# Where the weight tiles of the first outputs of a stage lie relative to h: other distances for gate/up and for queries, keys and values

## What is computed

```
for l in range(2):
    x = x + 0.5 * swiglu(rms_norm(x), wg1, wu1, wd1)      # wide: 2816
    h = rms_norm(x)
    z = h @ w_in                                          # q, k, v and three convolution parts
    x = x + concat(sliding_window_attention(q, k, v), short_conv(...)) @ w_out
    x = x + 0.5 * swiglu(rms_norm(x), wg2, wu2, wd2)
x = rms_norm(x)
```

## Time and profile before

| what | value |
|---|---|
| median of 3 launches | 1254.28 us |
| the three launches | 1238.87, 1262.2 and 1254.28 us |
| the profiled execution, its own time | 1245.92 us |
| its span, first to last instruction | 1244.1 us |
| mean granted clock of TensorE | 0.993 |
| TensorE matmuls, busy | 1202.5 us (97%) |
| TensorE weight loads, busy | 1161.1 us (93%) |
| VectorE, ScalarE, GpSimd busy | 816.5, 656.4 and 166.0 us |
| read from memory | 208.91 MB |

### The profile page before, as it was taken

One profiled execution on the slowest core, in us unless ns is written; L12 is line 12 of the kernel. 1 busy time (PEld: TensorE's weight loads), 2 busy tenths in 40 slices (PEclk: granted clock), 3 DMA queues, 4 the chain that ended last, 5 costly groups with the idle time before them and its releaser, 6 DMA issues.

```text
span 1244.1 us, 27307 instructions
## 1 busy us (share of the span) xinstructions
PE 1202.5 (97%) x10002; PEld 1161.1 (93%) x10002; DVE 816.5 (66%) x1390; ACT 656.4 (53%) x1121; POOL 166.0 (13%) x228
## 2 busy tenths in 40 slices
PE   6999999999999999999999999999997999998998
PEld 6999999799999999999999799999996887998888
DVE  6766654768666654777665868677656666655664
ACT  5454543556545544555543646555545665655652
POOL 3000000342000000000000351000000000401960
PEclk9999999999999999999999999999997999999999
DMA  7655753455555753655743446556652430543542
GB/s 281 200 180 191 230 175 113 143 166 191 184 187 185 239 166 117 202 189 189 252 167 136 136 159 196 190 195 216 212 169 75 137 126 20 168 155 128 179 153 86
DMA packets 56742, 210.91 MB, mean 170 GB/s; under 512 B 7200, under 2 KB 9280, under 8 KB 56544
## 3 DMA queue, kind: packets, MB, share of 16 engines
q1 hardware_dynamic: 54048, 203.45, 49.3%
q0 software_dynamic: 2480, 6.48, 1.8%
q10 hardware_dynamic: 144, 0.06, 0.0%
HBM read 208.91 MB, written 1.05 MB: 169 GB/s over the span
## 4 chain that ended last, share of the span: by engine, by line
PE 84%; DVE 7%; ACT 3%; issue 3%; POOL 2%; DMA 0%; DVEq 0%; ACTq 0%; SPq 0%
PE bank L1173 25%; PE bank L1175 25%; PE bank L1174 25%; DVE w_lo L748 3%; PE bank L1211 2%; PE bank L1520 2%; PE bank L1500 1%; DVE h_lo L767 1%; ACT w_hi L457 1%; PE bank L1485 1%; DVE probs L886 1%; PE bank L1422 1%; PE bank L1424 1%; PE bank L1423 1%; PE bank L1480 1%
## 5 line engine op out<-in xcount | busy, mean ns | idle before, releaser
L1173 PE MATMUL bank<-h_hi,w_hi 128*128 128x256 f32 (+1 forms) x1992 | 566.8, 285 | 16.8 <-DVE w_lo L748 11.6
L1175 PE MATMUL bank<-h_hi,w_lo 128*128 128x256 f32 (+1 forms) x1992 | 557.9, 280 | 0.0
L1174 PE MATMUL bank<-h_lo,w_hi 128*128 128x256 f32 (+1 forms) x1992 | 557.8, 280 | 0.0
L748 DVE TENSOR_TENSOR w_lo<-w_raw,w_hi 128x1024 fp32r<-128x1024 f32 (+1 forms) x360 | 467.7, 1303 | 75.1 <-ACT w_hi L457 74.9
L457 ACT ACTIVATE w_hi<-w_raw 128x1024 fp32r<-128x1024 f32 (+1 forms) x360 | 397.1, 1108 | 75.9 <-PE bank L1175 58.3
L1173 PEld LDWEIGHTS bank<-h_hi,w_hi 128*128 128x128 f32 x1992 | 377.1, 189 | 24.0 <-issue 19.4
L1175 PEld LDWEIGHTS bank<-h_hi,w_lo 128*128 128x128 f32 x1992 | 379.9, 191 | 0.0
L1174 PEld LDWEIGHTS bank<-h_lo,w_hi 128*128 128x128 f32 x1992 | 377.3, 189 | 0.9
L1173 PE MATMUL bank<-g_hi,w_hi 128*128 128x256 f32 x832 | 232.5, 279 | 1.5 <-DVE g_lo L893 0.8
L1174 PE MATMUL bank<-g_lo,w_hi 128*128 128x256 f32 x832 | 231.7, 278 | 0.0
L1175 PE MATMUL bank<-g_hi,w_lo 128*128 128x256 f32 x832 | 231.7, 278 | 0.0
(11 more groups left out here) (152 smaller groups left out, 1159.5 us busy)
## 6 DMA issues: line engine op xcount, KB each, us to landing
w_raw<-in_w SPq DMA_DIRECT2D x296, 512.0 KB, 3.3
w_raw<-in_wd SPq DMA_DIRECT2D x64, 704.0 KB, 4.1
w_raw<-in_relbias POOLq DMA_DIRECT2D x64, 64.0 KB, 2.3
btab_sb<-in_btab POOLq DMA_DIRECT2D x1, 1536.0 KB, 9.3
x_res<-in_xT SPq DMA_DIRECT2D x2, 512.0 KB, 4.9
out_T<-x_res SPq DMA_DIRECT2D x8, 128.0 KB, 1.7
rope_sb<-in_rope POOLq DMA_DIRECT2D x1, 272.0 KB, 3.9
mats_sb<-in_mats POOLq DMA_DIRECT2D x1, 192.0 KB, 3.8
```

What stands on the lines that cost most here:

```text
L748: dve.tensor_tensor(wlo[:, slot, at:at + cols], raw[:, slot, 0:cols], whi[:, slot, at:at + cols].bitcast(F32), ALU.subtract).then_inc(lo_r ...
L1173: pe.matmul(o, h, xh, start=first, stop=False)
L1174: pe.matmul(o, h, xl, start=False, stop=False)
L1175: return pe.matmul(o, lo, xh, start=False, stop=last)
```

## The change

The single shift `ASIDE` becomes a table by stage and output. `first_pair` is told which stage it works for, and output 2 of `gu1` and `gu2` is shifted too, at its splits and at its matmuls. The second block reads its first slots with the shifts of `gu1`.

```diff
-ASIDE = 56
+ASIDE = {('gu1', 1): 8, ('gu1', 2): 56, ('gu2', 1): 48, ('gu2', 2): 56, ('qkv', 1): 16}
 def tile_at(phase, i):
-    return ASIDE if phase in ("gu1", "gu2", "qkv") and i == 1 else 0
+    return ASIDE.get((phase, i), 0)
...
-            def first_pair(ready, q):
+            def first_pair(name, ready, q):
...
-                        mm = product(bank[o][:, 0:T], o, k, *hcols(k), k == 0, k == KT - 1, at=o * ASIDE)
+                        mm = product(bank[o][:, 0:T], o, k, *hcols(k), k == 0, k == KT - 1, at=tile_at(name, o))
...
-                            product(bank[1][:, 0:T], 1, k1, *hcols(k1), k1 == 0, False, at=ASIDE)
+                            product(bank[1][:, 0:T], 1, k1, *hcols(k1), k1 == 0, False, at=tile_at(name, 1))
...
-                first_pair(lambda r: ready(r, 0), q)
+                first_pair(name, lambda r: ready(r, 0), q)
                 for r in (2, 3):
                     ready(r, 0)
-                    tile8(bank[r][:, 0:T], r)
+                    tile8(bank[r][:, 0:T], r, at=tile_at(name, r))
...
-                                             at=a * ASIDE)
+                                             at=tile_at("gu1", a))
...
-                        mm = product(o[:, 0:TOKENS[kind]], slot, i, *hcols(i, TOKENS[kind]), i == 0, i == KT - 1)
+                        mm = product(o[:, 0:TOKENS[kind]], slot, i, *hcols(i, TOKENS[kind]), i == 0, i == KT - 1,
+                                     at=tile_at("gu1", 2) if piece == 2 else 0)
```

More of the change, by code:

```diff
@@ L1251, in qkv @@
             def qkv(l, q):
-                first_pair(lambda i: pe.wait_ge(lo_ready[PHASES["qkv"].slot(i)], uses("qkv", i, l)), q)
+                first_pair("qkv", lambda i: pe.wait_ge(lo_ready[PHASES["qkv"].slot(i)], uses("qkv", i, l)), q)
                 for i in range(2, QKV):
```

## The result

| | before | changed |
|---|---|---|
| median of 20 launches | 1249.98 us | 1250.02 us |
| lowest and highest | 1237.96, 1262.2 | 1245.16, 1261.93 |
| launches up to 1240 us | 5 | 0 |
| 1244 to 1248.2 us | 5 | 10 |
| 1251.8 to 1254.9 us | 7 | 9 |

What follows compares the result with a forecast made beforehand. TensorE, busy 97% of the span, was taken to be bound by the pace of matmul starts. From the profiled 1245.92 us, 13.6 off for all four stretches fast and 0.5 added for output 2 gave 1232.8, forecast as 1233 us; range 1229 to 1256.

Steps and rivals of the forecast that it cites:

- the two paces: Gate/up/down stretches from output 2 on: the same matmuls run at 0.1131 or 0.1176 us each, kept throughout the stretch.
- the price of a stretch: One slow gate/up/down stretch of 1536 matmuls costs 6.8 us over a fast one (180.70 against 173.90 us).
- the new second tile: Output 1 at 160, 0 or 128 bytes: if even, it fixes each stage's pace; bounds -13.6 to +13.6 us.
- all four (or all but a rare one) fast: Main case: all four gate/up/down stretches take the fast pace, giving 1233 us; chance 0.47.
- all slow: Rival: the regular handover leads to the slow pace in all four stretches, 1260.0 us; chance 0.09 for all or nearly all.
- gu1 as regular: Start of gu1: with output 1 even at its new distance, the handover comes in the same moment every time.
- One kind fixed fast, the other slow or open: Rival on gu1 and gu2: with two slow stretches 1246.4 us, with one 1239.6; chance 0.14.
- The draw stays a draw: Rival: nothing is fixed, each stretch is slow in 10 of 16 cases, 1249.8 us; chance 0.25.
- a slow window: Sign of being wrong: a window from output 3 on at 178 us in place of 171 us.
- the splits: ScalarE and VectorE writing the shifted tile at another address: taken as 0, with room to hide slower writes.
- the loads: Loads run at 196 to 201 GB/s in both paces, so they don't hold up a faster stretch.
- the waits: TensorE in the first block is hardly ever short of work; its two longest wait totals are 5.7 and 2.6 us.

Runs made afterwards that it cites:

- no_third: Changed kernel with the third tile of gu1 and gu2 back at 192 bytes; median 1256.69 us, ratio 1.0132 to the kernel before.
- pair_200: Second and third tiles of gu1 and gu2 at 200 bytes, second of qkv at 224; median 1232.37 us, ratio 0.9962 to the kernel before.
- changed_again: The changed kernel once more, beside the kernel before on a chip where that had 1237.32 us; median 1250.71 us, ratio 1.0104.
- the half change: Only gu1's part of the change (160 then 224 bytes), gu2 and qkv as in the kernel before; median 1239.77 us, ratio 0.9993.
- gu2_224: Changed kernel with gu2's second tile back at 224 bytes in place of 0; median 1242.99 us, ratio 1.003 to the kernel before.
- the pairs: Three kernels with second and third tiles of gu1 and gu2 at 32, 64 or 200 bytes, qkv's second at 224; medians 1233.06, 1233.3 and 1232.37 us.
- dist32_192: All gu1 tiles at 32 bytes, gu2 at 192, no tile set aside; one launch, within 1240.94 to 1259.96 us against 1241.01 for the kernel before.
- second_200: Kernel before with the second tile of gu1 and gu2 at 200 bytes in place of 224; median 1233.69 us against 1239.87, ratio 0.9947.

## Why the prediction was wrong

**Right: what bounds the kernel, and the two paces.** The change acts through nothing but the pace, there are two of them at 192 bytes, and a stretch keeps the one in which it starts. The twenty launches of before fall near the steps that the prediction took from three and a profile (their groups lie 6.9, 7.8 and 7.5 us apart; what the tenths beyond 6.7 are, no run shows).

**Right: the price of a stretch.** 6.8 us were forecast, for 1536 matmuls. The windows give 6.6 for the 1479 from output 3 on. Whole executions agree: no_third with four slow stretches took 1258.96 us and pair_200 with none 1232.04, which is 26.9 us or 6.7 a stretch. The floor of all four fast, forecast as 1232.8, was measured at 1230 to 1233 us, though with other distances than the change's.

**Right, and then misread: the new second tile.** "Were it even at the new distances, it would hand over in the same moment every time." In `gu2` it is even, at 0.120 us, and its outcome was the same in all 42 launches as far as their floor tells, and in the eight stretches profiled. The step that failed is the next one: that a regular handover would be a fast one, the -13.6 us of the sum and "all four (or all but a rare one) fast: 0.47". A regular handover fixes a pace, and nothing in the rows said which. The profiles have an even tile at 0.120 us on both sides: at 0 bytes all eight stretches behind it were slow, at 160 bytes (where it is even in six of sixteen stages profiled) all six were fast. The prediction had both signs as bounds (-13.6 and +13.6 us) and gave the good one the larger chance (0.47 against 0.09 for all slow) with no row that told them apart. At 0 bytes the fixed pace is the slow one, +2 x 6.6 us against a fast launch. Against the profiled execution, where the sum took 13.6 us off, two stretches are slow as before, and nothing came off (1245.92 and 1246.20 us).

**Wrong: gu1 as regular.** At 160 bytes the second tile has no single pattern. In the changed kernel's profile it was even at 0.120 us in layer 1 and uneven (0.119 in the mean) in layer 0. Over all profiles with a tile at 160 bytes, half of the ten stretches behind an uneven one were slow. In the launches the stretch behind it drew, read by the groups: of 20 launches 10 have just the two slow stretches of `gu2`, 9 have one more and 1 has two more, so 11 of 40 `gu1` stretches were slow, where the prediction counted 10 of 16 for the kernel before. So the change took away `gu2`'s odds, and `gu1`'s look better than before in these launches. Over them the kernel before has 1 x 5 + 2 x 5 + 3 x 7 + 4 x 3 = 48 slow stretches of 80 and the changed one 2 x 10 + 3 x 9 + 4 x 1 = 51. Three stretches of 6.6 us in 20 launches are 1.0 us on the mean, where 1.2 were measured, a difference that the scatter could also make by itself. Where the kernel before draws better, the fixed slow `gu2` costs more: 1.0104 in changed_again. How much of `gu1`'s better odds is the chip's I can't say: in the half change they brought no gain (0.9993), so that the change improves them isn't shown.

**The nearest rival.** "One kind fixed fast, the other slow or open", 1246.4 us with a chance of 0.14, had it the right way round for the slow kind: half of the launches lie at 1245.2 to 1248.2. The other half is the draw of `gu1` on top.

**Luck in a number.** "The draw stays a draw" gave 1249.8 us, and the median is 1250.02, inside the range that the prediction gave. For all four stretches that isn't the mechanism: two are fixed slow and two draw, and 1232.8 + 13.2 for `gu2` + 11 of 20 times 6.6 for `gu1` comes to 1249.6 us on the mean as well.

**The sign that it named.** What the text offered as sign of its being wrong, a slow window, came out as put. The launches lie 17 us apart (1245.16 to 1261.93) and not 3.

**Right at nothing:** the splits, the loads and the waits. (The loads of the earlier trace rows run at 192 to 201 GB/s; the prediction read 196.) TensorE waits as before, and the `qkv` stretch stayed fast in the changed kernel's first profile. It isn't immune: it was slow once in changed_again and once in gu2_224, both after the uneven tile at 128 bytes, and in all eight `qkv` stretches of the four kernels in which no `qkv` tile is shifted. The price is the 0.4 us that the prediction gave.

**The rule of the separate read ports.** The Trainium skill (TensorE: Matmul & The Clock Gate, Part 2, step by step) says that loading the next weights takes no read bandwidth from the running matmul. By it the shift would do nothing and the draw would stay. The runs speak against that, by the pace: 0.113 us at 192 bytes and 0.120 at 96, with the same instructions and clock. That the two reads meet somewhere in the memory is the obvious reading, but no run shows where, and it stays an argument.

**Left open:** whether it is the distance from h or the place of the weight tile by itself, since every run moves the tile and none moves h, so that both change by as much; why 200, 64 and 32 bytes hand over to the fast pace and 0 to the slow one; why the draw comes out so differently from one comparison to the next; and whether the pairs stay fast over many more launches than 12 each.

## What to carry to other kernels

Measure the pace of a saturated matmul stream by counting starts in a window, stretch by stretch. If it comes in two sizes, the spread between launches is a state and not noise, and a median over few launches compares draws: look at the floor and the groups of the launches instead. Where a state is set at a handover, a change that makes the handover regular can fix the bad state as well as the good one, so give both signs the same chance until a row tells them apart. Then try a few distances, each with a dozen launches, since one profile of a draw proves nothing.

## What the runs showed of the hardware

- Identical streams of 128x128 weights and 256 columns at full clock run at 0.1133 or 0.1178 us a matmul with the weights 192 bytes before h modulo 256, and keep their pace for 1479 matmuls.
- Where the weights lie against h moves the pace by up to 6%. Long streams ran at 0.113 at 192 bytes (dist32_192), 0.117 at 32, 0.118 at 64, 184, 200 and 208, 0.119 at 176, 0.120 at 96. At 64 bytes 0.1133 was seen as well, over two tiles.
- With 24 matmuls at 0 bytes at the start of `gu2` the 1479 others were slow in all eight stretches profiled. With 24 at 200 bytes (second_200) they were fast in all four, and no launch of 12 was above 1235.24 us.
- How often a handover comes out fast depends on the chip or its moment: the kernel before had a median of 1249.98 us over the first 20 launches and 1237.3 to 1239.9 us in the later comparisons; the profiled execution of the first had a mean clock of 0.993, most launches of the later ones 0.992 to 0.994.
